# Expert stage of a decoder step: rows gathered in quarters and turned on VectorE, gate and up weights loaded in quarters, TensorE's order changed

## The reference

```python
def routed_expert_mlps(x, expert_ids, gates, w_gate, w_up, w_down):   # x: (2112, 1024), two experts of 64 per token
    ...                                                    # tokens sorted by expert into blocks of MOE_BLOCK = 128
    def expert_block(args):
        tb, eb = args                                      # tokens of the block, its expert
        xb = x[tb]
        h = jax.nn.silu(xb @ w_gate[eb]) * (xb @ w_up[eb]) # w_gate, w_up: (64, 1024, 256)
        return h @ w_down[eb]                              # w_down: (64, 256, 1024)
    ...                                                    # results scaled by the gates and added to their tokens
```

## Time and profile before

| | |
|---|---|
| time, median of 3 runs | 2602.05 us (2592.71 to 2602.96) |
| the profiled execution, its own time | 2603.91 us |
| its span | 2602.2 us |
| busy of the span: TensorE, VectorE, ScalarE, GpSimd | 90%, 39%, 27%, 18% |
| gate and up products L3056, 1024 instructions | 446.6 us busy |
| down products L3072, 512 instructions | 236.0 us busy |
| turns of x L3043, 528 instructions | 72.3 us busy |
| gathers L2762 and scatters L2807 on GpSimd | 68 and 66, 1.0 us each |
| bytes read and written in DRAM | 345.1 and 94.8 MB |

### The profile page before, as it was taken

How to read it: one execution, slowest core, us unless ns; L and a number is a source line. 1 busy time by engine, 2 the same in 40 slices (tenths; PEclk the granted TensorE clock), 3 DMA queues, 4 the chain that set the end, 5 groups by cost and what they waited for, 6 DMA issues and landing times. The chain is left out here.

```text
span 2602.2 us, 36339 instructions
## 1 busy us (share of the span) xinstructions
PE 2333.2 (90%) x13208; PEld 1339.2 (51%) x13208; DVE 1027.2 (39%) x1762; ACT 707.5 (27%) x1825; POOL 456.6 (18%) x632
## 2 busy tenths in 40 slices
PE   7999999999968999999999999849999999999940
PEld 3454454533546666666667666524444444444420
DVE  4415234224226554456656656341111211112128
ACT  3203122012025544345444554201111111111112
POOL 1010100100200011200131311212222212212235
PEclk9999999999978999899999999969999999999975
DMA  8041230400373112121122111167999999999967
GB/s 283 26 134 33 57 103 9 131 11 11 97 226 76 56 61 88 52 65 56 56 79 88 56 56 61 60 250 297 367 362 361 363 369 370 361 362 361 354 249 314
DMA packets 165971, 440.35 MB, mean 169 GB/s; under 512 B 36961, under 2 KB 78169, under 8 KB 141225
## 3 DMA queue, kind: packets, MB, share of 16 engines
q1 hardware_dynamic: 139351, 350.38, 37.7%
q0 software_dynamic: 20640, 70.29, 6.8%
q10 hardware_dynamic: 5842, 17.80, 1.8%
HBM read 345.11 MB, written 94.80 MB: 169 GB/s over the span
## 5 line engine op out<-in xcount | busy, mean ns | idle before, releaser
L867 PE MATMUL p_ps<-p_xt,p_w 128*128 128x512 f32 x1088 | 476.7, 597 | 0.5 <-DVE p_xt L698 0.5
L3056 PE MATMUL p_ps<-p_w_arena,p_x_arena 128*128 128x512 f32 x1024 | 446.6, 594 | 0.0
L867 PEld LDWEIGHTS p_ps<-p_xt,p_w 128*128 128x128 f32 x1088 | 205.2, 191 | 255.2 <-issue 250.0
L3056 PEld LDWEIGHTS p_ps<-p_w_arena,p_x_arena 128*128 128x128 f32 x1024 | 195.5, 191 | 245.4 <-issue 245.4
L2426 PE MATMUL p_ps<-p_w_out,p_mixt 128*128 128x512 f32 x544 | 252.5, 609 | 0.0
L3072 PE MATMUL p_ps<-p_w_arena,p_y_arena 128*128 128x512 f32 x512 | 236.0, 604 | 0.0
L2978 DVE SCALAR_TENSOR_TENSOR p_y_arena<-p_y_arena,p_ps 128x256 f32<-128x256 f32 x64 | 27.0, 422 | 459.9 <-ACT p_y_arena L2863 358.2
L2426 PEld LDWEIGHTS p_ps<-p_w_out,p_mixt 128*128 128x128 f32 x544 | 99.6, 193 | 105.8 <-issue 103.7
L876 PE MATMUL p_ps<-p_w,p_xt 128*128 128x144 f32 (+1 forms) x512 | 146.6, 440 | 0.0
L2807 POOL DMA_INDIRECT s_y<-p_y_arena,p_home x66 | 65.0, 985 | 462.3 <-PE p_ps L3043 266.6
L3072 PEld LDWEIGHTS p_ps<-p_w_arena,p_y_arena 128*128 128x128 f32 x512 | 93.1, 192 | 98.2 <-issue 93.0
(11 more groups left out here) (415 smaller groups left out, 3254.1 us busy)
## 6 DMA issues: line engine op xcount, KB each, us to landing
p_w_arena<-in_w_exp_gate SPq DMA_DIRECT2D x64, 1024.0 KB, 7.9
p_w_arena<-in_w_exp_up SPq DMA_DIRECT2D x64, 1024.0 KB, 11.1
p_w_arena<-in_w_exp_down SPq DMA_DIRECT2D x64, 1024.0 KB, 10.6
p_w_arena<-s_y SPq DMA_DIRECT2D x16, 1024.0 KB, 13.3
p_x<-in_x_prompt SPq DMA_DIRECT2D x30, 512.0 KB, 4.8
p_w<-in_w_in SPq DMA_DIRECT2D x4, 2048.0 KB, 15.5
p_spread<-s_roots SPq DMA_DIRECT2D x16, 512.0 KB, 7.1
s_kv<-p_us SPq DMA_DIRECT2D x32, 256.0 KB, 2.3
```

What stands on the lines that cost most here:

```text
L867: ins = mm(ps[:, job % 4, :], w[:, c, at:at + P], xt[s % 2][:, c, :], start=(c == 0), stop=(c == KC - 1))
L3056: t = mm(ps[:, 2 + b, :], xt[b][:, c, :], w_gu[bw][:, :, c, :], start=(c == 0), stop=(c == KC - 1))
```

## The change

- Gate and up weights of a block come in four DMAs each, one for each quarter of 32 partitions, in place of one. Partition 32 q + a holds rows 32 a + 8 q + c of the weights. `hn` is written in the columns' order that answers to this, and the router's weights are loaded in quarters too (8 DMAs for 2).
- A block's x comes in four indirect DMAs, for quarters of the lanes: on partition 32 k + r, columns 256 g to 256 g + 255 get quarter k of the row of lane 32 g + r. The numbers for that are made once in `moe` by four products with a 0/1 matrix (`sel`, `spread`), and in `gather_listed` from four more small loads of the list.
- VectorE turns x in squares of 32x32 in one instruction (`turn_x`), from SBUF to SBUF. TensorE's turns of x, and ScalarE's and VectorE's copies of them, are gone.
- Empty lanes have a number out of bounds and are skipped by gather and scatter. x is cleared once at the start by GpSimd.
- TensorE: the turn of the first block's mid stands in the middle of the second block's gate and up, the second's between the halves of the first block's down. The freed banks of PSUM give mid and y of both blocks banks of their own.

The diff, cut to its core:

```diff
@@ mix_prompt
-                    (w_route[:, :, 0:NG], A["w_router_group"][0].rearrange("(p c) n -> p c n", p=P)),
-                    (w_route[:, :, NG:], A["w_router_expert"][0].rearrange("(p c) n -> p c n", p=P))]
+        WEIGHTS += [(w_route[32 * j:32 * j + 32, :, cols], A[name][0].rearrange("(a c j) n -> j a c n", c=KC, j=4)[j])
+                    for cols, name in ((slice(0, NG), "w_router_group"), (slice(NG, NR), "w_router_expert")) for j in range(4)]
...
-                stt(hn[:].rearrange("p c q -> p q c"), h[:].rearrange("p (q c) -> p q c", c=KC), hr[:],
+                stt(hn[:].rearrange("p c q -> p (c q)").rearrange("p (b a) -> p a b", a=32), h[:].rearrange("p (a b) -> p a b", a=32),
@@ moe, SP
-                    sp.dma_start(w_gu[b][:, t].rearrange("p c f -> p (c f)"),
-                                 src[bass.ds(e, 1)].rearrange("o (p c) f -> p (o c f)", p=P)).then_inc(arrived[b], 16)
+                    for q in range(4):
+                        sp.dma_start(w_gu[b][32 * q:32 * q + 32, t].rearrange("a c f -> a (c f)"),
+                                     src[bass.ds(e, 1)].rearrange("o (a q c) f -> q a (o c f)", q=4, c=KC)[q]).then_inc(arrived[b], 16)
@@ moe, GpSimd
-                pool.indirect_dma_start(out=x[b], out_offset=None, in_=S["hn"],
-                                        in_offset=bass.IndirectOffsetOnAxis(ap=slot[b][:, 0:1], axis=0)
-                                        ).then_inc(x_in[b], 16)
+                for g in range(4):
+                    apart(pool, on["slots_ready"], 1)
+                    pool.indirect_dma_start(out=x[b][:, 256 * g:256 * g + 256], out_offset=None,
+                                            in_=S["hn"].rearrange("t (q k) -> (t q) k", q=4),
+                                            in_offset=bass.IndirectOffsetOnAxis(ap=slot[b][:, g:g + 1], axis=0),
+                                            bounds_check=4 * NTOK - 1, oob_is_err=False).then_inc(x_in[b], 16)
...
-                    pool.dma_start(raw[n][:], S["ids"][bass.ds(q, 1)].rearrange("o c -> c o")).then_inc(raw_in[n], 16)
+                    pool.dma_start(raw[n][:, 0:1], S["ids"][bass.ds(q, 1)].rearrange("o c -> c o")).then_inc(raw_in[n], 16)
+                    for k in range(4):
+                        pool.dma_start(raw[n][32 * k:32 * k + 32, 1:5],
+                                       S["ids"][bass.ds(q, 1)].rearrange("o (g b) -> b (o g)", g=4)).then_inc(raw_in[n], 16)
...
-                                        in_=y[b], in_offset=None).then_inc(y_out[b], 16)
+                                        in_=y[b], in_offset=None, bounds_check=2 * HOMES + P - 1, oob_is_err=False
+                                        ).then_inc(y_out[b], 16)
...
+            nc.gpsimd.memset(x_arena[:, 0:R * D], 0.0).then_inc(on["x_cleared"], 1)
+            pool.wait_ge(on["x_cleared"], 1)
@@ moe, VectorE
-                nc.vector.tensor_copy(xt[b][:, 0:4, :], ps[:, 0, :].rearrange("p (c t) -> p c t", c=4)
-                                      ).then_inc(xt_vec.sem, 1)
+            def turn_x(j, b, bx, x_count):
+                dve.wait_ge(x_in[bx], x_count)
+                dve.wait_ge(gu_done.sem, gu_done.back(j, 2))
+                nc.vector.transpose(xt[b].rearrange("p c (g r) -> p g c r", g=4), x[bx].rearrange("p (g c a) -> p g c a", g=4, c=KC)
+                                    ).then_inc(xt_ready.sem, 1)
@@ moe, TensorE
+            for g in range(4):
+                t = mm(ps[:, 4, g * NE:(g + 1) * NE], sel[:, g].rearrange("p q b -> p (q b)"), token, start=True, stop=True)
+            t.then_inc(on["spread"], 1)
...
-                        turn(j + 2, b, (bw + 2) % R, 4 * i + (16 if half_ == 0 else 32))
...
+                        if b == 0:
+                            gate_up(j, b, bw, range(KC))
+                        else:
+                            gate_up(j, b, bw, range(KC // 2))
+                            turn_mid(j - 1, 0)
+                            gate_up(j, b, bw, range(KC // 2, KC))
+                    j, bw = i + half_, half_
+                    pe.wait_ge(midt_ready.sem, midt_ready.all(j))
+                    pe.wait_ge(down_in[bw], 4 * i + 16)
+                    down(j, 0, bw, 0)
+                    turn_mid(j + 1, 1)
+                    down(j, 0, bw, 1)
+                    pe.wait_ge(midt_ready.sem, midt_ready.all(j + 1))
+                    pe.wait_ge(down_in[bw + 1], 4 * i + 16)
+                    down(j + 1, 1, bw + 1, 0)
+                    down(j + 1, 1, bw + 1, 1)
```

More of the change, by code:

```diff
@@ L99, in constants @@
     room = PLACES * P * np.arange(NE)
-    c["spare"] = (2 * HOMES + 1 + i)[:, None]
+    spare = np.where(i > 0, float(ABSENT), 2.0 * HOMES + 1)
+    c["spare"] = np.stack([spare, np.where(i % 32 > 0, float(ABSENT), 4.0), i // 32], 1)
     c["route"] = np.concatenate([
@@ L2653, in moe @@
         owner = sb("owner", [1, 2 * SPILL + 1], I32)
[L2654 to L2658, removed]
+        homes = sb("homes", [P, SLOTS], I32)
+        slots = K["lg"][:].rearrange("p t n -> p (t n)")[:, 0:4 * NE].rearrange("p (g e) -> p g e", g=4)
+        sel = cut(work, 9 * D, (4, 4, 32))
+        slot = [sb(f"slot{b}", [P, 4], I32) for b in ring]
+        raw = [sb(f"raw{b}", [P, 5]) for b in two]
+        home_f, token_f, none_f = sb("home_f", [P, 1]), sb("token_f", [P, 4]), sb("none_f", [P, 4])
+        spare = sb("spare", [P, 3])
         home = [sb(f"home{b}", [P, 1], I32) for b in two]
@@ L2787, in gather_listed, with step @@
-                apart(pool, on["slots_ready"], 1)
-                nc.gpsimd.tensor_scalar(home_f[:], home_f[:], -1.0, None, ALU.add).then_inc(step_own.sem, 1)
-                nc.gpsimd.tensor_scalar(slot[b][:], token_f[:], -1.0, 0.0, ALU.add, ALU.max).then_inc(slot_ready.sem, 1)
-                pool.wait_ge(step_own.sem, step_own.all(j + (R - NE)))
-                apart(pool, on["slots_ready"], 1)
+                def step(k):
+                    pool.wait_ge(step_own.sem, step_own.part(j + (R - NE), k))
+                    apart(pool, on["slots_ready"], 1)
@@ new lines, in gather_listed @@
+                ts(quad, quad, 4.0, -4.0, ALU.mult, ALU.add).then_inc(step_own.sem, 1)
+                step(6)
+                tt(home_f[:], home_f[:], raw[n][:, 0:1], ALU.add).then_inc(step_own.sem, 1)
+                tt(token_f[:], token_f[:], quad, ALU.add).then_inc(step_own.sem, 1)
+                tt(none_f[:], none_f[:], spare[:, 2:3].to_broadcast([P, 4]), ALU.add).then_inc(step_own.sem, 1)
+                step(9)
+                ts(home_f[:], home_f[:], -1.0, None, ALU.add).then_inc(step_own.sem, 1)
@@ L2792, in gather_listed @@
+                tt(token_f[:], token_f[:], none_f[:], ALU.add).then_inc(step_own.sem, 1)
+                step(11)
                 nc.gpsimd.tensor_copy(homes[:, bass.ds(j, 1)], home_f[:]).then_inc(homes_own.sem, 1)
+                nc.gpsimd.tensor_copy(slot[b][:], token_f[:]).then_inc(slot_ready.sem, 1)
                 pool.wait_ge(homes_own.sem, homes_own.all(j + (R - NE)))
@@ L2989, in _ @@
-            evacuate_x(0, 0)
-            evacuate_x(1, 1)
-            with dve.Fori(0, NE - R, 2) as i:
+            def turn_x(j, b, bx, x_count):
[3 more added lines that the diff above has]
+                                    ).then_inc(xt_ready.sem, 1)
+            def blocks(i):
+                for half_ in range(0, R, 2):
+                    for b in two:
+                        j = i + half_ + b
+                        dve.wait_ge(th_ready.sem, th_ready.all(j))
+                        dve.wait_ge(midt_turned.sem, midt_turned.back(j, 2))
+                        nc.vector.scalar_tensor_tensor(mid[b], th[b], 1.0, ps[:, 2 + b, 0:DE], ALU.add, ALU.mult
+                                                       ).then_inc(mid_own.sem, 1)
+                        dve.wait_ge(mid_own.sem, mid_own.all(j))
+                        nc.vector.scalar_tensor_tensor(mid[b], mid[b], 0.5, ps[:, 2 + b, DE:], ALU.mult, ALU.mult
+                                                       ).then_inc(mid_ready.sem, 1)
+                        turn_x(j + 2, b, (half_ + b + 2) % R, 16 * i + (64 if half_ == 0 else 128))
+                    for b in two:
+                        j = i + half_ + b
+                        dve.wait_ge(down_done.sem, down_done.part(j, 1))
+                        dve.wait_ge(y_out[b], 8 * i + (16 if half_ == 0 else 32))
+                        nc.vector.tensor_copy(y[b][:, 0:512], ps[:, 0 if b else 5, :]).then_inc(y_vec.sem, 1)
```

160 lines of the change are left out of this document (68 added, 92 removed).

## The result

The kernel after takes 2961.82 us, median of four runs (2956.14 to 2977.95), against 2600.78 for the kernel before beside it (2592.71 to 2602.96): 1.1405 times as long, 95% interval 1.1353 to 1.1456. The forecast of 2682 us, range 2595 to 2750, had the sign and the first cause, and missed the size by 280 us.

A forecast was written before the change was run, and what follows sets the result against it. The prediction took TensorE as the nearer bound, then half-rate weight loads at 12.8 us a block: listed rounds begin at 2448, plus 146 for them, plus 85.9 after the last scatter, span 2680, forecast 2682 us, range 2595 to 2750.

The forecast's parts named there:

- T: Expert stage: DMA time of a block, 10.0 + 2.6 + 0.2 = 12.8 us, from 12.5 to 14.6.
- C: End: GpSimd's chain of eight listed rounds, forecast 146 us (115 to 175), against 103.3 in the kernel before.
- Gate and up at half rate: Expert stage: quarter loads of gate and up run at 210.5 GB/s, as w_out's halves did, 10.0 us a block.
- Down "at full 0.410": Expert stage: the down load, still whole over 128 partitions, runs at full rate, 2.6 us a block.
- Gather and scatter "hidden", 0.2 us: Expert stage: rows and y move beside the half-rate loads, 0.2 us a block; paid in full, 1.3 to 2.0.
- rival 4: Expert stage: gather and scatter not hidden, T = 14.6, 2778 us; fetching absent lanes anyway, 2751 us; chance 0.12.
- Skipped lanes "cost nothing or gain": Expert stage: with empty lanes skipped, gather and scatter each fall to 0.270 MB a block and may cost nothing.
- TensorE 10.6 a block: Expert stage: without the turns of x, TensorE needs 21.2 us a pair, 10.6 a block, against 11.5 before.
- Rival 1: Expert stage: quarter loads overlap, half rate doesn't hold, TensorE's 10.6 us a block decides: 2609 us, chance 0.12.
- VectorE's turn: Expert stage: turning 128x1024 in squares takes 1.28 to 1.96 us and, with some 10 us of room, costs nothing.
- Clearing x: Start: GpSimd's clearing of x, some 4 x 1.3 us, lies under the routing and costs nothing; 5 us if uncovered.
- The listed rounds: End: each of eight GpSimd rounds grows 7.2 us, a late one 9.2 to 16.4; 15 us off for a lighter queue.

The follow-up runs named there:

- after_step: Kernel after, with SyncE issuing a block's down load only once that block's gate and up have landed: 2935.65 us, 16.6 us a block.
- before_halves: Kernel before, with gate and up weights each loaded as two DMAs of 64 partitions: 2848.96 us, 15.5 us a block.
- after_alternate: Kernel after, with the quarter loads issued in the order 0, 2, 1, 3: 2936.55 us, 16.9 us a block.
- before_quarters: Kernel before, with gate and up weights each loaded as four DMAs of 32 partitions: 2828.76 us, 15.5 us a block.
- after_no_down: Kernel after without the down loads of blocks 4 to 63, so y is not the reference's: 2710.74 us, 11.95 us a block in the steady stage.
- whole: Kernel after, but with gate and up weights each in one DMA of 128 partitions and VectorE's turn reading with a stride of 8: 2607.36 us, 1.0044 times before.
- before_four: Kernel before, with gate and up weights each in four DMAs over all 128 partitions, a quarter of the columns each: 2594.12 us, against 2596.94 for before.

## Why the prediction missed

Where the prediction failed is T, the DMA time of a block: 12.8 us (12.5 to 14.6) for 17.1 measured. The step was to sum each load at the rate that it has by itself, with down at full rate and rows and y at 0.2. The sum against the span of 2976.3, in its own terms: start of the listed rounds 2706 for 2448 (+258), C = 182 for 146 (+36), from the last scatter at 2888.3 to the end 88.0 for 85.9 (+2).

- **Gate and up at half rate: right.** Lined up, the quarters move 205 to 229 GB/s (after_step), against the 210.5 of w_out, and halves of the partitions are as slow. The 10.0 us stands. The Trainium skill, page "SBUF — State Buffer", section "Door 1: The DMA port swizzle", has 189 GB/s for partitions 0 to 31; the rate here is higher. Its section "Can I just issue two DMAs to hit both halves?" has a gain of 6% for two DMAs to the two halves; before_halves (2848.96) and after_alternate (229 GB/s for 223) agree that the halves together help little.
- **Down "at full 0.410": the step that failed.** Beside quarter loads it is seen in before_quarters (430) and in after_step (418). In the kernel after even the start has no more than 294 and 329 GB/s (windows from 1722 to 1726 and from 1766 to 1770), and from 1900 to 2600 two windows of 700 pass 350. There a down load costs 5.2 us (after_no_down), 2.6 more than the sum had. I took each DMA's rate by itself, as if SP's queue ran one DMA after the other. That it does so only while its engines are at the same place is my explanation; shown is that the loss goes with the scatter's skipping and ends where down has no quarter load beside it.
- **Gather and scatter "hidden", 0.2 us: wrong too.** Without any down load a block takes 11.95 us, 2.0 over the 10.0 of gate and up, and before_quarters takes 15.5 for a sum of 15.2 with every byte paid. So they are paid in full; the 1.3 to 2.0 that I put at the other end, and into rival 4, was the value. Of the 4.3 us a block some 1.8 are this and 2.5 the down load (an estimate, from after_no_down). The two together passed the top of my range, 14.6, which had rows and y at 2.0 and down at full rate.
- **Skipped lanes "cost nothing or gain": the sign was wrong**, and no rival had it. Undoing the skipping gives 38 us back with 0.5 MB more a block, adding it to before_quarters costs 145. Fewer bytes were counted; what they do to the loads beside them was not.
- **TensorE 10.6 a block: right**, 10.55 in whole. Rival 1, the half rate lifted, had 2609 us; whole, which has no half rate, takes 2607.36. In part that is luck: its listed rounds begin 10 us earlier than the rival had them (2365.3 for 2375), C is 6 longer and the tail 2. VectorE's turn takes 1.24 us in after, just under the range 1.28 to 1.96, and is hidden.
- **The rest of the 258 us.** The 43 blocks from block 13 to 56 make 43 x 4.3 = 185. If the ten before them lost as much each, 43 more, 30 are left, and they aren't split up further here. Some lie at the start: the first product is at 1754.73; the list scatters end at 1815.4 for 1806, block 3's mid is turned only at 1826.52 and block 4's products begin at 1833.29 for 1819. Five of the eight list scatters wait 6 to 9.5 us for the one before, in the kernel before at most 5.9, and the eight take 10 us longer. VectorE waits in its new turn for x of block 4 (38.63 us, to 1824.46) and holds up TensorE's turn of mid behind it, which I had not named. Some lie at the other end: block 56's products begin at 2692.10, and block 55 is sent only at 2703.83, its scatter having waited 7.38 us for the one before. The rows of the start:

```profile
1793.46 0.95 POOL L2843 DMA_INDIRECT s_ids<-p_h_all,p_place_i  x1 [8.36 <-DMA s_ids<-p_h_all,p_place_i]
```

```profile
1826.52 0.70 PE L3077 MATMUL p_ps<-k_ident,p_y_arena 128*128 128x128 f32 x2 [33.28 <-DVE p_y_arena L3004]
```

- **Clearing x: right.** It took 3.51 us at 1728.01, done long before the numbers were ready at 1740.08.
- **The listed rounds.** A late one takes 17.1 us (2838.79 to 2855.91) for 16.4. The first ones are what was mis-sized: I took 15 us off for a lighter queue, and it got heavier. GpSimd's waits for the list loads in the first two rounds, in after and then in before:

```profile
2723.12 0.24 POOL L2791 TENSOR_SCALAR p_home_f<-p_raw 128x1 f32<-128x1 f32 x1 [14.13 <-DMA p_raw<-s_ids]
...
2753.70 0.24 POOL L2791 TENSOR_SCALAR p_home_f<-p_raw 128x1 f32<-128x1 f32 x1 [16.05 <-DMA p_raw<-s_ids]
```

```profile
2419.74 0.24 POOL L2775 TENSOR_SCALAR p_home_f<-p_raw 128x1 f32<-128x1 f32 x1 [6.12 <-DMA p_raw<-s_ids]
2440.68 0.23 POOL L2775 TENSOR_SCALAR p_home_f<-p_raw 128x1 f32<-128x1 f32 x1 [11.56 <-DMA p_raw<-s_ids]
```

In whole, with the weights at full rate, these waits are 5.79 and 6.40 us and C is 2516.9 - 2365.3 = 152. So 30 of the 36 us come again with the quarter loads.

## What to carry to other kernels

A load into a part of the partitions can slow more than itself: count every transfer that can stand beside it at its rate, and pay side traffic in full where DMA is the bound. Fewer bytes are not a gain by themselves: here a scatter that skipped its last lanes cost more than the bytes saved. And when a bound moves from one engine to another, look first at the last rounds: there 0.9 us a block over the whole stage was given back, and cutting four useless rounds brought it out.

## What the runs showed of the hardware

- Weights loaded into 32 or 64 partitions at a time made a block take 15.5 us either way, where with loads over all 128 TensorE sets the pace at 11.5, and four DMAs over all 128 in place of one cost nothing (before_quarters, before_halves, before, before_four).
- Skipping on the mean 62 of 128 lanes of a block's gather and scatter cost 145 us in all beside quarter loads (2828.76 to 2973.68), and nothing visible beside full ones.
- An indirect DMA takes GpSimd 1.0 us with 128 rows of 4 KB (1.03 for the scatter in the earlier trace rows) and with quarter rows of 1 KB (mean 1019 ns, 272 of them), most of the latter skipped in the last two of each four.
- One VectorE instruction turns 128x1024 float32 in squares in 1240 ns in after; in whole, whose input is read with a stride of eight elements, it takes 2027 ns (of whole's costliest groups):

```profile
L2990 DVE STREAM_TRANSPOSE p_x_arena<-p_x_arena 128x1024 f32<-128x1024 f32 x66 | 133.8, 2027 | 122.0 <-DMA p_x_arena<-s_hn,p_slot 122.0
```
